# Moving the output-gate projections of a recurrent layer between the levels of its recurrence, with SiLU built from tanh

## The reference, cut to what matters

```python
def _hgrn2(h, lb, w_in, out_norm, w_out):
    ...
    z = h @ w_in
    q_pre = z[..., :F]
    f_pre = z[..., F:2 * F]
    i_in = z[..., 2 * F:2 * F + E]
    g_pre = z[..., 2 * F + E:]
    f = lb + (1.0 - lb) * jax.nn.sigmoid(f_pre.astype(jnp.float32))
    log_f = jnp.log(f)
    k = 1.0 - f
    q = jax.nn.silu(q_pre.astype(jnp.float32))
    v = i_in.astype(jnp.float32)
    ...
    def step(state, inp):
        qc, kc, vc, lfc = inp
        b = jnp.cumsum(lfc, axis=2)
        o_inter = jnp.einsum('bhtd,bhde->bhte', qc * jnp.exp(b), state)
        diff = b[:, :, :, None, :] - b[:, :, None, :, :]
        decay = jnp.where(causal, jnp.exp(jnp.where(causal, diff, 0.0)), 0.0)
        a = jnp.einsum('bhtd,bhsd,bhtsd->bhts', qc, kc, decay)
        o_intra = jnp.einsum('bhts,bhse->bhte', a, vc)
    ...
    o = o * lax.rsqrt(jnp.mean(o * o, axis=-1, keepdims=True) + NORM_EPS)
    o = o.reshape(B, S, E) * out_norm.astype(jnp.float32) * jax.nn.silu(g_pre.astype(jnp.float32))
    return o.astype(h.dtype) @ w_out
```

## Time and profile before

| what | value |
|---|---|
| median of three runs | 3083.33 us (3080.94 to 3085.2) |
| the profiled execution, as timed | 3083.25 us |
| its span in the trace, first to last instruction | 3081.2 us |
| PE busy over the span | 98% |
| mean granted clock of PE | 0.981 of full speed |
| the `hg_g` projections | 43.51 us (1571.23 to 1614.74) |
| the recurrence, from its first matmul to the first of `hg_out` | 147.5 us (1658.23 to 1805.70) |

### The profile page before, as it was taken

How to read it: one execution, slowest core, us unless ns; L and a number is a source line. 1 busy time by engine, 2 the same in 40 slices (tenths; PEclk the granted TensorE clock), 3 DMA queues, 4 the chain that set the end, 5 groups by cost and what they waited for, 6 DMA issues and landing times.

```text
span 3081.2 us, 43953 instructions
## 1 busy us (share of the span) xinstructions
PE 3013.4 (98%) x16132; PEld 2662.8 (86%) x16132; DVE 2354.5 (76%) x4427; ACT 1202.7 (39%) x1879; POOL 1317.2 (43%) x749
## 2 busy tenths in 40 slices
PE   7999999999999999999999999999999999999998
PEld 5658899999998888888788888999999997888887
DVE  5345899998987888888335647899888968888887
ACT  4433333444443333333434433334444434333333
POOL 3303465443434444443345433465444435443442
PEclk9899999999999999999998789999999999999999
DMA  3203266999999999998221003367999999999996
GB/s 137 74 14 103 95 200 243 340 376 356 376 365 383 361 361 356 351 357 325 94 96 62 1 28 110 115 206 279 358 359 370 366 367 378 367 351 347 365 352 254
DMA packets 345718, 800.83 MB, mean 260 GB/s; under 512 B 27937, under 2 KB 191777, under 8 KB 345249
## 3 DMA queue, kind: packets, MB, share of 16 engines
q1 hardware_dynamic: 271776, 529.55, 49.3%
q0 software_dynamic: 73728, 268.47, 23.0%
HBM read 695.15 MB, written 102.76 MB: 259 GB/s over the span
## 4 chain that ended last, share of the span: by engine, by line
PE 91%; DVE 3%; DMA 3%; issue 1%; ACT 1%; SPq 0%; POOL 0%; DVEq 0%; ACTq 0%
PE PS L1449 28%; PE PS L1451 27%; PE PS L1450 27%; PE PS L1617 3%; DMA arena<-acts_dram 1%; PE PS L1688 1%; PE PS L1594 1%; PE PS L1555 1%; DMA gates_dram<-arena 1%; PE PS L1572 1%; PE PS L1554 1%; PE PS L1730 0%; PE PS L1691 0%; PE PS L1562 0%; PE PS L1707 0%
## 5 line engine op out<-in xcount | busy, mean ns | idle before, releaser
L1449 PE MATMUL PS<-x_hi,w_hi 128*128 128x384 f32 (+1 forms) x2616 | 924.4, 353 | 15.2 <-issue 7.5
L611 ACT ACTIVATE w_hi<-w_raw 128x1024 fp32r<-128x1024 f32 x609 | 643.3, 1057 | 684.3 <-PE PS L1451 671.6
L1451 PE MATMUL PS<-x_hi,w_lo 128*128 128x384 f32 (+1 forms) x2616 | 907.9, 347 | 0.0
L1450 PE MATMUL PS<-x_lo,w_hi 128*128 128x384 f32 (+1 forms) x2616 | 906.7, 347 | 0.0
L550 POOL DMA_INDIRECT arena<-in_v_t,arena x256 | 445.8, 1741 | 600.1 <-DVE resid L1238 550.1
L1449 PE MATMUL PS<-w_hi,x_hi 128*128 128x512 f32 x1744 | 679.4, 390 | 5.5 <-DVE x_lo L1255 5.4
L1451 PE MATMUL PS<-w_hi,x_lo 128*128 128x512 f32 x1744 | 678.6, 389 | 0.0
L1450 PE MATMUL PS<-w_lo,x_hi 128*128 128x512 f32 x1744 | 678.5, 389 | 0.0
L539 POOL TENSOR_TENSOR w_lo<-w_raw,w_hi 128x1024 fp32r<-128x1024 f32 x169 | 419.1, 2484 | 572.8 <-ACT w_hi L611 572.7
L1215 DVE TENSOR_TENSOR w_lo<-w_raw,w_hi 128x1024 fp32r<-128x1024 f32 x440 | 537.3, 1221 | 109.1 <-ACT w_hi L611 104.5
L550 POOL DMA_INDIRECT arena<-in_u_rows,arena x256 | 381.1, 1489 | 487.1 <-DVE arena L1222 433.8
(11 more groups left out here) (183 smaller groups left out, 2421.4 us busy)
## 6 DMA issues: line engine op xcount, KB each, us to landing
w_raw<-in_u_t SPq DMA_DIRECT2D x256, 512.0 KB
w_raw<-in_v_t SPq DMA_DIRECT2D x256, 512.0 KB
acts_dram<-arena SPq DMA_DIRECT2D x256, 192.0 KB
gates_dram<-arena SPq DMA_DIRECT2D x24, 2048.0 KB
arena<-gates_dram SPq DMA_DIRECT2D x64, 768.0 KB
arena<-acts_dram SPq DMA_DIRECT2D x256, 192.0 KB
w_raw<-in_hg_t SPq DMA_DIRECT2D x40, 512.0 KB
w_raw<-in_pq_t SPq DMA_DIRECT2D x32, 512.0 KB
```

The costliest lines, as they stand in the source:

```text
L611: act.activation(w_hi[:, slot, :], w_raw[:, slot, :], ACT.Copy).then_inc(hi_ready, 1)
L1449: pe.matmul(ps, wh, xh, start=start, stop=False)
L1450: pe.matmul(ps, wh, xl, start=False, stop=False)
L1451: return pe.matmul(ps, wl, xh, start=False, stop=stop)
```

## The change

The gate's tiles move behind the values' tiles in `STREAM`, in the host's weight array and on PE. Gate 0 is projected after `hg_i`, before the recurrence. The blocks of gates 1 to 7 are put between the levels: behind `a` of step n, for n from 4 to 45, two blocks (6 matmuls) at four steps of six, so that gate h occupies steps 6h - 2 to 6h + 1. All gates use PSUM bank 6. ACT takes the tanh of half the gate (it was a Silu), and DVE computes (tanh + 1) times the gate, at step 6h + 3; the missing factor 0.5 is put into the output gain beforehand. The high and low parts of the tiles move along: POOL splits `hg_g` tiles 2, 3, 4 and 5 behind steps 6, 9, 11 and 14, and a tile every six steps after that, the last four being those of `hg_out`.

```diff
 STREAM = [...
-          ("hg_q", 8), ("hg_f", 8), ("hg_g", 8), ("hg_i", 8), ("hg_out", 8),
+          ("hg_q", 8), ("hg_f", 8), ("hg_i", 8), ("hg_g", 8), ("hg_out", 8),
...
+def gate_parts(h, p):
+    n = 8 * h + p
+    return 2 if 4 <= n < 6 * HEADS - 2 and (n - 4) % 6 < 4 else 0
+
+def gate_finished(n):
+    return n // 6 if n % 6 == 3 and n // 6 < HEADS else None
+
 def recurrence():
+    part = 0
+    while part < KC:
+        yield "gate", 0, part
+        part += 1
...
                 yield "spread", SPREAD_AT[h, p], 0
+            for k in range(gate_parts(h, p)):
+                yield "gate", part // KC, part % KC
+                part += 1
...
-    eight("hg_i", BASE["hg_i"] + 7, "act", (2, 3, 0, 1, 4, 5, 6, 7))
+    eight("hg_i", BASE["hg_i"] + 7, "act", (2, 3, 6, 0, 1, 4, 5, 7))
...
+        elif what == "gate":
+            if p == 0:
+                b.add(("hg_g", h), "gate", BASE["hg_g"] + h, (6,))
...
-                               "ho": ("act", None, (6, 7)), "hss": ("sum", None, (5,))}[what])
+                               "ho": ("act", None, (7,)), "hss": ("sum", None, (5,))}[what])
...  POOL
-            lows(BASE["hg_q"], BASE["hg_i"] + 8)
+            lows(BASE["hg_q"], BASE["hg_g"] + 2)
...  ACT
-            for n in range(8):
-                ready(act, ("hg_g", n))
-
-                free(act.activation(gg_[:, n, :], PSb(("hg_g", n)), ACT.Silu), ("hg_g", n))
-                next_high(BASE["hg_g"] + n)
...
+            next_high(BASE["hg_i"] + 4)
+            next_high(BASE["hg_i"] + 5)
+
+            def gate_tanh(h):
+                ready(act, ("hg_g", h))
+                act.activation(gg_[:, h, :], PSb(("hg_g", h)), ACT.Tanh, scale=0.5).then_inc(sem("gate_tanh"), 1)
+                next_high(BASE["hg_g"] + h)
...
-                    if h == 1 and k % 2 == 0:
-                        next_high(BASE["hg_i"] + 4 + k // 2)
+                    if (h, k) in ((0, 2), (0, 3)):
+                        next_high(BASE["hg_i"] + 4 + k)
+                    if gate_finished(8 * h + k) is not None:
+                        gate_tanh(gate_finished(8 * h + k))
...  DVE
+            out_gain = gain[:, G_AT["out"]:G_AT["out"] + HEADS]
+            chain(dve.tensor_scalar(out_gain, out_gain, 0.5, None, ALU.mult))
...
+            def gate_silu(h):
+
+                dve.wait_ge(sem("gate_tanh"), h + 1)
+                free(dve.scalar_tensor_tensor(gg_[:, h, :], gg_[:, h, :], 1.0, PSb(("hg_g", h)), ALU.add, ALU.mult),
+                     ("hg_g", h))
...
+                if gate_finished(n) is not None:
+                    gate_silu(gate_finished(n))
...  PE
-            for name in ("hg_q", "hg_f", "hg_g"):
+            for name in ("hg_q", "hg_f"):
...
+                elif what == "gate":
+
+                    n = BASE["hg_g"] + h
+                    w = slice(p * P, (p + 1) * P)
+                    if p == 0:
+                        wait_low(pe, n)
+                        begin(("hg_g", h))
+                    mm = three(PSb(("hg_g", h)), w_hi[:, n % RING, w], w_lo[:, n % RING, w], x_hi[:, p, :],
+                               x_lo[:, p, :], p == 0, p == KC - 1)
+                    if p == KC - 1:
+                        end(mm, ("hg_g", h))
```

More of the change, by code:

```diff
@@ L123, in __init__ @@
         self.signals = 0
-        self.count = {"act": 0, "dve": 0, "exp": 0, "state": 0, "kd": 0, "sum": 0, "spread": 0}
+        self.count = {"act": 0, "dve": 0, "exp": 0, "state": 0, "kd": 0, "sum": 0, "spread": 0, "gate": 0}
         self.turn, self.last = {}, {}
@@ L225, in plan @@
         b.add(("hg_f", n), "act", BASE["hg_f"] + n)
-    for n in range(8):
-        b.add(("hg_g", n), "act", BASE["hg_g"] + n)
-    eight("hg_i", BASE["hg_i"] + 7, "act", (2, 3, 0, 1, 4, 5, 6, 7))
+    eight("hg_i", BASE["hg_i"] + 7, "act", (2, 3, 6, 0, 1, 4, 5, 7))
     for what, h, p in recurrence():
@@ L358, in model @@
         ps_ready, tile_used = sem("ps_ready"), sem("tile_used")
-        freed = {who: sem(f"{who}_freed") for who in ("act", "dve", "exp", "state", "kd", "sum", "spread")}
+        freed = {who: sem(f"{who}_freed") for who in ("act", "dve", "exp", "state", "kd", "sum", "spread", "gate")}
         hi_ready, pool_low, dve_low = sem("hi_ready"), sem("pool_low"), sem("dve_low")
@@ L589, in _ @@
                 take_diff(n)
-                if n in range(11, 11 + 2 * RING, 2):
-                    lows(BASE["hg_out"] + (n - 11) // 2, BASE["hg_out"] + (n - 11) // 2 + 1)
+                if n in (6, 9, 11):
+                    lows(BASE["hg_g"] + n // 3, BASE["hg_g"] + n // 3 + 1) if n < 11 else                         lows(BASE["hg_g"] + RING, BASE["hg_g"] + RING + 1)
+                elif n >= 14 and n % 6 == 2 and (n - 8) // 6 < HEADS:
+                    lows(BASE["hg_g"] + RING + (n - 8) // 6, BASE["hg_g"] + RING + (n - 8) // 6 + 1)
             lows(BASE["hg_out"] + RING, BASE["u1"] + FIRST_GATHER)
@@ L1811 @@
     hg = a["hg_w_in"][0]
-    hg_t = cat([_across_tiles(hg[:, :2 * DM]), _across_tiles(hg[:, 3 * DM:]),
-                hg[:, 2 * DM:3 * DM].reshape(8, P, DM), a["hg_w_out"][0].reshape(8, P, DM)], 0)
+    hg_t = cat([_across_tiles(hg[:, :2 * DM]), hg[:, 2 * DM:3 * DM].reshape(8, P, DM),
+                _across_tiles(hg[:, 3 * DM:]), a["hg_w_out"][0].reshape(8, P, DM)], 0)
     pq_t = np.stack([_across_tiles(w) for w in a["peer_w_q"]])
```

## The result

The changed kernel takes 3061.02 us (median of 4 runs, 3058.05 to 3062.27), the kernel before 3083.1 us in the same measurement; the ratio is 0.993, with a 95% interval of 0.992 to 0.994. The prediction was 3059 us, with a range of 3045 to 3074. In a second measurement the ratio was 0.991 (0.989 to 0.993).

A forecast was written before the change was run, and what follows sets the result against it. The prediction took PE to bound the kernel: -38.1 us for the gates leaving, +12.1 for steps 0 to 43, +1.5 for the rest, -24.5 us in sum, from 3083.25 to 3059 us; 8-in-10 range 3045 to 3074.

The forecast's parts named there:

- The seven gates leave: Gate stage before the recurrence: 7 of 8 gates leave it, 7/8 of 43.51 us, -38.1 us.
- PE's need at full clock, 93.9 us, and the turns, 2.5: Steps 0 to 43: 55.8 us plus 38.1 of blocks; 28 turns to 128x512 matmuls at 0.09 us, 2.5 us.
- The start: Before level 4 of head 0: PE waits 3.4 us, as ACT has three high parts and a tanh before the exponentials.
- Steps without blocks: Pairs 8-9 to 38-39: DVE slower than PE but ahead, 0.25 us a pair, 1.5 in all; step 27, 2 more.
- crowding on POOL and ACT: Steps 6 to 14: four of POOL's ten low parts fall there; no engine becomes the bound, 2 us added.
- Clock: Steps 0 to 43: full clock expected nearly throughout thanks to dense matmuls behind 28 of 40 steps; 2.5 us allowed.
- The last 20 steps: Steps 44 to 63: no blocks, slow clock as before; two low parts and gate 7's silu are new, +1.5 us.
- The clock did not stay low: Slower rival, steps 0 to 43: clock stays at 0.71, stretch 138 us, total 3089 us; chance 5%.
- rival 2: Steps 0 to 43: clock 0.87, every other head falls once, stretch 119 us, total 3070 us; chance 20%.
- Rival 4: Recurrence: new ring of waits among tiles' low and high parts, tanh and PE; 2.4 us x 7, total 3076; chance 5%.
- Rival 3: Steps 0 to 43: blocks fit better, 4 us of loss, total 3048 us; last 20 steps could start warmer; chance 15%.
- The signs: Profile after: steps 0 to 43 103 to 113 us, clock over 0.93, idle below 12; steps 44 to 63 51 to 55.

The follow-up runs named there:

- second execution: The changed kernel measured once more, without a further edit, on the chip of the kernel with tanh, high part and silu one step later: 3054.07 us, ratio 0.991.

## Why the prediction was right, point by point

- **The seven gates leave, -38.1 us.** Measured -38.0. `hg_i` took their place with no wait (43.55 us at clock 1.00), and the sums of the logarithms were hidden, as told.
- **PE's need at full clock, 93.9 us, and the turns, 2.5.** The kernel with the extra matmuls shows the stretch with the rest taken away: 98.5 us at clock 1.00, with 1.5 us of waits; the sum was 96.4. This step, on which the prediction stood, holds within 1%. The split of the 39.9 us that were lost before was less exact: the earlier trace rows has PE idle for 95.67 - 86.25 = 9.4 us, not some 12, so that slow clock was some 30.
- **The start, 3.4 us.** Measured 0.83 + 1.88 = 2.7, in front of levels 3 and 4 of head 0, for the reason given. The changed kernel's timeline has the three high parts and the tanh there.
- **Steps without blocks, 1.5 + 2 us, and crowding on POOL and ACT, 2.** This is the step that failed. The prediction reasoned that DVE comes out of four steps with blocks ahead of PE and stays so. It left out that ACT waits at the tanh for the end of the gate, and that the round of the next levels stands behind it, on ACT and then on DVE. Measured to step 43 are 2.27 + 1.60 + 1.86 + 2.27 = 8.0 us for the four waits, 10.7 with the start against 8.9 in the sum. The size is near by luck: the 2 us for step 27 are there (1.86 before step 28), for the reason that I gave for that step, and four gates more have a wait like it, whose start is the tanh's own. Behind gates 1 and 5 the head's own matmuls (`kd`, `values`, `ho`) cover it.
- **Clock, 2.5 us.** Too small: 0.10 of 118.5 is 11.8, and 0.07 of 115.5, in the second execution, 8. It comes with these waits and not with the levels: with the waits gone it is 0.98 and 1.00, without any tanh 1.00. 96.4 + 10.7 + 11.8 = 118.9, measured 118.5, predicted 107.8.
- **The last 20 steps, +1.5 us.** The sign was wrong: they became shorter, 51.4 to 44.1 us. PE's busy time for the same matmuls fell from 44.3 to 38.3 us with the mean clock at 0.88 instead of 0.77, 6 of the 7 us. This offset 8.8 of the 10.7 us by which steps 0 to 43 were missed, and that is why the total came so close: two misses of opposite sign, which is luck. The reason is not settled. A full clock on entry is not enough, as the kernel with half of the extra matmuls enters at 1.00 and needs 51.3; nor are steps 44 and 45 back to back behind a block, as the kernels with the high part alone later and with Silu enter so and need 49.9 and 50.4. Where no extra matmuls stand in these steps, their lengths are of two kinds only, 43 to 44 us at 0.88 or 50 to 51 at 0.77 to 0.80, and two executions of one kernel agreed in it.
- **The rivals.** The clock did not stay low (0.90, above the 0.76 at which all would have been paid back), and rival 2, with a mean of 0.87 in the stretch, is what that stretch alone came near to: 119 us predicted there, 118.5 measured. The forecast and that rival differ by 11 us in the total, and the last 20 steps decided between them. Rival 4 named the place, tanh and high part in ACT's order waiting for PE, but put it to the tiles arriving late; no wait of PE for a `w_lo` shows in the trace, and its chance of 5% was too low for what it described. Rival 3 had said that the last 20 steps could start warmer; they became shorter, though the blocks did not fit better.
- **The signs.** PE's idle time in steps 0 to 43 is 10.7 us, below the 12 named, and the matmuls of a gate stand 0.23 us apart. But the stretch of 118.5 us lies outside the 103 to 113, its clock of 0.90 below the 0.93, and the last 20 steps outside their 51 to 55. The total stands within its range while the working for these stages does not.
- **The rule of the pages.** The Trainium skill, page "TensorE: Matmul & The Clock Gate", section "A second HAM failure mode: psum-queue depth-cycling", has the clock swing under small idle times between groups, where they are frequent enough. The kernel before agrees: 16 waits of 0.25 to 1.1 us in steps 0 to 43, and clock 0.71. The runs do not bear out what the prediction made of the rule, that blocks would not mend it: with them waits are few, 6 in the changed kernel (0.90 and 0.93), 6 in the one with half the extra matmuls and 4 in the one with all (1.00 in both).

## What to carry to other kernels

Where PE idles between short matmuls, price work that is put there with the clock in the sum: here 19 us of added matmuls made the stretch 13 us shorter, and 38 us cost 2. Work that is moved between the steps of a round of engines brings its drain with it. Ask, for each engine in order, where it stands when the moved work ends: an instruction that waits for that end cancels the lead of all that is queued behind it. Placing it one step later can keep the lead; here that shortened the recurrence by 16 to 18 us. And compare a forecast with its result stage by stage: here the total was right while two stages were 9 to 11 us off, in opposite directions.

## What the runs showed of the hardware that I had not expected

- Matmuls whose result nobody reads made the kernel no slower: 168 of them left it at a ratio of 0.999 (0.998 to 1.000), with the recurrence at 141.6 instead of 147.5 us; 84 of them gave 0.997 (0.996 to 0.998) and 134.6 us.
- 84 matmuls in 28 of 44 steps were enough for a granted clock of 1.00 over the stretch that had 0.71 (steps 0 to 43).
- The length of a wait did not decide alone whether the clock fell. The kernel before has its 0.71 with no wait above 1.1 us. In the changed kernel those of 2.27 and 1.86 us had matmuls at the lower level behind them, those of 1.60 and 1.59 us had not; in the kernel with the high part later one of 1.51 us had (the 8 matmuls behind it took 1.95 us), in the one with half the extra matmuls one of 1.68 us had not, and in the one with Silu not even one of 2.99 us (8 matmuls in 1.11 us, the fall came within the block behind them). What decides is not settled by these runs.
